# Moved norm, first-slot and band work in a two-layer decoder trunk, and two weight forms rounded in one instruction

## The reference

```
x = x + 0.5 * swiglu(rmsnorm(x, n_ffn1), w_gu, w_down)     # d_ff = 2816
x = x + mixer(rmsnorm(x, n_mix))           # layer 0: gated linear attention, layer 1: windowed means
x = x + cross_attention(rmsnorm(x, n_xattn), rmsnorm(mem, n_mem))
x = x + 0.5 * swiglu(rmsnorm(x, n_ffn2), w_gu, w_down)
```

## Time and profile before

| | |
|---|---|
| median of three runs | 1996.6 us |
| the profiled execution | 1997.72 us |
| its span, first to last instruction | 1995.6 us |
| TensorE (PE) busy | 1962.7 us, 98% |
| VectorE (DVE) busy | 1183.7 us, 59% |
| ScalarE (ACT) busy | 841.5 us, 42% |
| GpSimd (POOL) busy | 182.9 us, 9% |
| granted TensorE clock, mean | 0.995 |

### The profile page before, as it was taken

One profiled execution on the slowest core, in us unless ns is written; L12 is line 12 of the kernel. 1 busy time (PEld: TensorE's weight loads), 2 busy tenths in 40 slices (PEclk: granted clock), 3 DMA queues, 4 the chain that ended last, 5 costly groups with the idle time before them and its releaser, 6 DMA issues. The chain is left out here.

```text
span 1995.6 us, 27296 instructions
## 1 busy us (share of the span) xinstructions
PE 1962.7 (98%) x10622; PEld 1703.2 (85%) x10622; DVE 1183.7 (59%) x1595; ACT 841.5 (42%) x1249; POOL 182.9 (9%) x213
## 2 busy tenths in 40 slices
PE   9999999999999989999999899999999999999998
PEld 7888888888898878989998798899798888888887
DVE  5343343587765668947966895698487544434323
ACT  5222232265554545524544563365256443322222
POOL 2000001100112120001001100100322122200000
PEclk9999999999999999999999999999999999999999
DMA  5323352323434532333333233333353424432222
GB/s 175 105 89 100 100 143 77 102 64 106 128 126 132 164 89 80 100 100 106 105 95 106 64 105 103 98 106 100 89 185 123 106 85 127 158 105 92 97 95 74
DMA packets 250063, 214.77 MB, mean 108 GB/s; under 512 B 22802, under 2 KB 232848, under 8 KB 249984
## 3 DMA queue, kind: packets, MB, share of 16 engines
q1 hardware_dynamic: 226304, 192.95, 31.2%
q0 software_dynamic: 6432, 17.64, 3.4%
q10 hardware_dynamic: 17248, 3.16, 0.9%
HBM read 203.23 MB, written 10.49 MB: 107 GB/s over the span
## 5 line engine op out<-in xcount | busy, mean ns | idle before, releaser
L2134 DVE TENSOR_TENSOR w_lo<-raw,w_hi 128x512 fp32r<-128x512 f32 (+5 forms) x283 | 410.2, 1450 | 368.4 <-ACT w_hi L1446 368.2
L1446 ACT ACTIVATE w_hi<-raw 128x512 fp32r<-128x512 f32 (+5 forms) x283 | 344.3, 1229 | 263.9 <-PE ps L429 259.1
L427 PE MATMUL ps<-h_hi,w_hi 128*128 128x512 f32 (+1 forms) x1088 | 420.3, 386 | 0.5 <-DVE w_lo L2134 0.5
L428 PE MATMUL ps<-h_lo,w_hi 128*128 128x512 f32 (+1 forms) x1088 | 418.6, 385 | 0.0
L429 PE MATMUL ps<-h_hi,w_lo 128*128 128x512 f32 (+1 forms) x1088 | 418.1, 384 | 0.0
L427 PEld LDWEIGHTS ps<-h_hi,w_hi 128*128 128x128 f32 x1088 | 205.7, 189 | 41.1 <-DVE w_lo L2134 0.9
L429 PEld LDWEIGHTS ps<-h_hi,w_lo 128*128 128x128 f32 x1088 | 205.7, 189 | 40.7
L428 PEld LDWEIGHTS ps<-h_lo,w_hi 128*128 128x128 f32 x1088 | 205.8, 189 | 39.6
L1034 PE MATMUL ps<-s_hi,w_hi 128*128 128x256 f32 x640 | 181.5, 284 | 3.7 <-DVE ps L2235 2.0
L1035 PE MATMUL ps<-s_lo,w_hi 128*128 128x256 f32 x640 | 181.1, 283 | 0.0
L1036 PE MATMUL ps<-s_hi,w_lo 128*128 128x256 f32 x640 | 181.1, 283 | 0.0
(11 more groups left out here) (411 smaller groups left out, 3436.1 us busy)
## 6 DMA issues: line engine op xcount, KB each, us to landing
raw<-in_ffn_w_gu SPq DMA_DIRECT2D x88, 512.0 KB, 5.0
raw<-in_ffn_w_gu SPq DMA_DIRECT2D x43, 1024.0 KB, 5.1
raw<-in_ffn_w_down SPq DMA_DIRECT2D x18, 1024.0 KB, 5.1
raw<-in_x_w_kv SPq DMA_DIRECT2D x16, 1024.0 KB, 6.0
raw<-in_ffn_w_down SPq DMA_DIRECT2D x20, 768.0 KB, 4.4
raw<-in_gla_w_in SPq DMA_DIRECT2D x12, 1024.0 KB, 5.2
raw<-in_ffn_w_down SPq DMA_DIRECT2D x16, 640.0 KB, 4.2
raw<-in_x_w_q SPq DMA_DIRECT2D x8, 1024.0 KB, 5.2
```

Of the source, the lines that this page charges most:

```text
L427: nc.tensor.matmul(out_ap, left[0], right[0], start=first, stop=False)
L428: nc.tensor.matmul(out_ap, left[0], right[1], start=False, stop=False)
L1446: return nc.scalar.activation(out_ap, in_ap, ACT.Copy, **kw)
L2134: return nc.vector.tensor_tensor(out_ap, value, hi.bitcast(F32), ALU.subtract)
```

## The change

- **Norm.** In the last step of feed_last_pairs the split of the next weights and the split of the sums come first, then the sums of x.
- **First slots.** POOL's weight_sums is gone; VectorE makes these three sums (with the two plain slots in a first half, ahead of the last down pair's split for a second half). The high and low parts of the second plain slot's chunk move behind the first slot's silu. In slot 0 seed_fourth moves ahead of P1's form of the next slot.
- **Two forms in one.** w_sums is laid out anew so that P5 and P6 lie side by side; one instruction on ScalarE and one on VectorE round both (two_forms). In the other slots seed_fourth stands between sum_three and the pair. P4's form moves from place 6 to 7.
- **Ends of halves.** The first down slot is split as soon as P6 of the last slot is done (it was P2), the second after P3 (it was the last product), both earlier in the lists. The wait for low_gated moves from ahead of half_down's loop to its second block.
- **Bands.** band_split moves from ahead of the down weights to behind the second pair of them.

```diff
-    SPOT = {P1: 0, P5: 1, P6: 2, P2: 3, P7: 4, P3: 5, P4: 6}
-    SUM_OF = {P5: 0, P7: 1, P6: 2, P4: 3}
+    SPOT = {P1: 0, P5: 1, P6: 2, P2: 3, P7: 4, P3: 5, P4: 7}
+    SUM_OF = {P5: 0, P6: 1, P7: 2, P4: 3}
...
@@ gpsimd
-            weight_sums(1, 0)
-            weight_sums(1, 1)
             add_squares(4)
-            weight_sums(2, 0)
-            weight_sums(2, 1)
             bands()
@@ tensor, half_down
-                pe.wait_ge(sig.mixed_dve_step, dve_step(end - 1, C12_TAKEN))
...
+                                if (pair, g, c) == (0, 0, 1):
+                                    pe.wait_ge(sig.mixed_dve_step, dve_step(end - 1, C12_TAKEN))
@@ scalar
+            def two_forms_hi(m, done_sem, done):
+
+                w = mixed_slots[m]
+                act.wait_ge(sig.w_sum_ready, OPENED + 3 * m + SUM_STEP[P6])
+                act.wait_ge(done_sem, done)
+                hi_part(two_forms(w_hi, w), w_sums[:, 0:2]).then_inc(sig.form_hi_ready, 2)
@@ scalar, feed_last_pairs
                     feed(f, 7)
+                    split_next(split_after)
+                    sums_hi(f)
                     scale_x(f, 2)
-                    split_next(split_after)
                     x_sums_hi(f, 2)
                     scale_x(f, 3)
-                    sums_hi(f)
                     x_sums_hi(f, 3)
@@ scalar, mixed_run
                     if following:
-                        for i in (P5, P6):
-                            form_hi(m + 1, i, sig.product_done, product_count(m, i))
+                        two_forms_hi(m + 1, sig.product_done, product_count(m, P6))
...
+                    if not following:
+                        split_hi(w % 2, area[w], loaded[w], product_count(m, P6), slot_rows[w], sig.product_done)
...
+                split_hi((w + 1) % 2, area[w + 1], loaded[w + 1], product_count(m, P3), slot_rows[w + 1],
+                         sig.product_done)
                 high_silu(m, s)
-                split_hi((w + 1) % 2, area[w + 1], loaded[w + 1], OPENED + PRODUCTS * end, slot_rows[w + 1],
-                         sig.product_done)
@@ scalar and vector, mixed_ffn
-                    if (n, part) == (2, 1):
-                        band_split()
...
+                        if (n, part, pair) == (2, 1, 1):
+                            band_split()
@@ vector
+            def two_forms_lo(m):
+
+                w = mixed_slots[m]
+                dve.wait_ge(*form_hi_count(m, P6))
+                lo_part(two_forms(w_lo, w), w_sums[:, 0:2], two_forms(w_hi, w)).then_inc(sig.form_lo_ready, 2)
@@ vector, mixed_run
                         if s == 0:
+                            sum_columns(m0)
+                            sum_three(m0)
+                            sum_four(m0)
                             split_next(at["gu", n, 0].slot)
...
-                        half_mid_lo(s)
+                        if s == 0:
+                            half_mid_lo(0)
...
                     if following:
                         sum_columns(m + 1)
+                        if l == 0:
+                            seed_fourth(m, s, b)
                         form_lo(m + 1, P1)
                         sum_three(m + 1)
-                        form_lo(m + 1, P5)
-                    seed_fourth(m, s, b)
+                    if l > 0:
+                        seed_fourth(m, s, b)
                     if following:
-                        form_lo(m + 1, P6)
+                        two_forms_lo(m + 1)
...
-                    if l > 0:
-                        half_mid_lo(s - 1)
-                    high_up(m, s, b)
-                    w = mixed_slots[m] + 1
-                    if following:
+                        if l > 0 or part == 0:
+                            half_mid_lo(s - 1)
+                        high_up(m, s, b)
                         form_lo(m + 1, P7)
                     else:
                         split_lo(w % 2, area[w], w + 1, slot_rows[w])
+                        high_up(m, s, b)
+                        half_mid_lo(s - 1)
@@ vector, mixed_ffn
+                        if (part, pair) == (0, 3):
+                            sum_columns(mixed_first[n, 1])
+                            sum_three(mixed_first[n, 1])
+                            sum_four(mixed_first[n, 1])
```

More of the change, by code:

```diff
@@ L443, in form, with two_forms @@
             return flat.rearrange("p (k n) -> p k n", n=P)
+        def two_forms(parts, w):
+            spot = SPOT[P5] + 4 * area[w]
+            flat = parts[:].rearrange("p s k n -> p (s k n)")[:, spot * KH * P:(spot + 2) * KH * P]
+            return flat.rearrange("p (f k n) -> p f k n", f=2, n=P)
         def dve_step(m, step):
@@ L720, in turn_x @@
                 pool.dma_start(final_gain[:], io.n_final.unsqueeze(0).broadcast_to([P, D])).then_inc(sig.gain_loaded, 16)
[L722 to L737, removed]
             def store_o(h):
@@ L1086, in last_block @@
                 banks, _ = mixed_banks(n, part)
-                pe.wait_ge(sig.form_lo_ready, OPENED + 6 * end)
+                pe.wait_ge(sig.form_lo_ready, form_count(end, P4))
                 pe.wait_ge(sig.mixed_dve_step, dve_step(end - 1, C22_READY))
@@ L1457, in split_next @@
                     if w + 2 in mixed_slots:
-                        for i in LEADING:
-                            form_hi(mixed_slots.index(w + 2), i, sig.part_done, slot_end[w])
+                        first = mixed_slots.index(w + 2)
+                        form_hi(first, P1, sig.part_done, slot_end[w])
+                        two_forms_hi(first, sig.part_done, slot_end[w])
+                        form_hi(first, P2, sig.part_done, slot_end[w])
                         return
@@ L1521, in half_mid_hi, with plain_mid_hi @@
                     hi_part(half_hi[:, s % HALF, :], t[:, s % 2, :]).then_inc(sig.mid_hi_ready, 1)
+                def plain_mid_hi(s):
+                    act.wait_ge(sig.evacuated, at["gu", n, s].out + 2)
+                    hi_part(half_hi[:, s, :], t[:, s, :]).then_inc(sig.mid_hi_ready, 1)
                 if part == 0:
@@ L1530, in mixed_run @@
                         else:
-                            act.wait_ge(sig.w_sum_ready, OPENED + 3 * m0 + SUM_STEP[P4])
                             for i in (P7, P3):
                                 form_hi(m0, i, sig.part_done, before_run)
-                        act.wait_ge(sig.evacuated, o_gate + 2)
-                        hi_part(half_hi[:, s, :], t[:, s, :]).then_inc(sig.mid_hi_ready, 1)
+                        if s == 0:
+                            plain_mid_hi(0)
                 else:
-                    act.wait_ge(sig.w_sum_ready, OPENED + 3 * m0 + SUM_STEP[P4])
                     for i in (P7, P3):
@@ L1541, in mixed_run @@
                     m, s = m0 + l, l + (PLAIN_FIRST, HALF)[part]
-                    following = m + 1 < end
+                    following, w = m + 1 < end, mixed_slots[m] + 1
                     act.wait_ge(sig.product_done, product_count(m, P1))
@@ L1571, in mixed_run @@
                         half_mid_hi(m - 1, s - 1)
+                    elif part == 0:
+                        plain_mid_hi(1)
                     if following:
                         form_hi(m + 1, P7, sig.product_done, product_count(m, P7))
-                    else:
-                        split_hi(w % 2, area[w], loaded[w], product_count(m, P2), slot_rows[w], sig.product_done)
+                split_hi((w + 1) % 2, area[w + 1], loaded[w + 1], product_count(m, P3), slot_rows[w + 1],
+                         sig.product_done)
                 high_silu(m, s)
-                split_hi((w + 1) % 2, area[w + 1], loaded[w + 1], OPENED + PRODUCTS * end, slot_rows[w + 1],
-                         sig.product_done)
                 half_mid_hi(m, s)
@@ L2147, in split_next @@
                     if w + 2 in mixed_slots:
-                        for i in LEADING:
-                            form_lo(mixed_slots.index(w + 2), i)
+                        first = mixed_slots.index(w + 2)
+                        form_lo(first, P1)
+                        two_forms_lo(first)
+                        form_lo(first, P2)
                         return
@@ L2163, in sum_columns @@
                 dve.wait_ge(raw_loaded[w % 2], loaded[w])
-                dve.wait_ge(*form_lo_count(m - 1, P7))
-                nc.vector.tensor_tensor(w_sums[:, 0:2], *outer_columns(w), ALU.subtract).then_inc(sig.w_sum_ready, 1)
+                if m > 0:
+                    dve.wait_ge(*form_lo_count(m - 1, P7))
+                nc.vector.tensor_tensor(w_sums[:, 0:3:2], *outer_columns(w), ALU.subtract).then_inc(sig.w_sum_ready, 1)
             def sum_three(m):
                 dve.wait_ge(sig.w_sum_ready, OPENED + 3 * m + 1)
-                nc.vector.tensor_tensor(w_sums[:, 2], quarter(mixed_slots[m], 1, 1), w_sums[:, 0], ALU.subtract)\
+                nc.vector.tensor_tensor(w_sums[:, 1], quarter(mixed_slots[m], 1, 1), w_sums[:, 0], ALU.subtract)\
```

(12 more changed lines are left out.)

2 lines of the change are left out of this document (removed).

## The result

The changed kernel takes **2004.95 us** (median of five runs, 2004.38 to 2005.96) against 1996.6: ratio 1.0043 [1.0029, 1.0057], slower by 8.6 us [5.8, 11.4] (1996.6 times what the ratio is above one). Forecast were 1998.9. Its profiled execution has a span of 2003.4 us, 7.8 more than before, at a mean granted clock of 0.996.

What follows compares the result with a forecast made beforehand. TensorE, busy 98%, bounds the kernel, with VectorE close behind and becoming the slots' bound. Runs +9.8, ends of halves -3.6 and bands -3.9 sum to +2.3 us on 1996.6: 1998.9, range 1995 to 2003.

Steps and rivals of the forecast that it cites:

- The slot: In each slot, the pair's wait makes VectorE's round 10.46 us against TensorE's 10.08, a cost of 0.38 us each.
- Norms and first slots: Norm waits go, new waits replace most; P1 of slot 1 comes 2.2 us earlier in the first run, 1.8 in the second.
- the wait for P1's form: In the first slots behind the norms, TensorE now stands idle 4.4 us for this form.
- The wait for ScalarE's copy: Ahead of P6 in the first slots, TensorE stands idle 3.2 us for ScalarE's copy of bank 6.
- rival 3: In two first slots, low clock lasts through P6, delaying product and seed 0.8 to 1.2 us: 2001; chance 0.05.
- Ends and bands: Earlier splits gain 0.9 us at each of four half ends, 3.6 in all; moving the bands' split gains 3.9.
- Rival 1: In the slots, the pair's wait is hidden and TensorE stays the bound: 1985.1 us; chance 0.20.
- Rival 2: In the slots, TensorE resumes 0.4 us slower, keeping a 0.2 us wait before P3 in 32 rounds: 2005.3; chance 0.20.

## Why the prediction was wrong

**The slot.** Right in its mechanism: VectorE is the bound of the slots, through the wait of the pair. Wrong in the size of one step, "Now: sum_three 0.68 us, 0.04, the high part of 128x1024 in 1.06 us, 0.04, and only then the pair's low part: 1.82 us". The two hand-overs of 0.04 us were read from instructions that raise their counter by one. The diff has `then_inc(..., 2)` on both of the new ones, and it costs 0.05 and 0.07: 1.93 us and a round of 10.57 in place of 10.46. Over 32 rounds that is 32 x 0.11 = 3.5 us, where the range had allowed 0.05 us a round, and the kernel with the count mended is 3.9 us faster by its median. The prediction had read the diff for operations and waits, and not for what an instruction does to its counter.

**What is left.** With the count mended the sum is +2.5 us by stages, forecast +2.3. By the medians it is +4.0 (2001.06 against 1997.05), and its ratio, [1.0013, 1.0031], lies a little above the forecast's 1.0012. The execution profiled there was the fastest of its ten (1999.51), and that of the kernel before (1997.72) was 1.1 us over its median, so these two traces differ by less than the medians do. Of the 6.1 us between 1998.9 and 2004.95 some 4 are the step above; the other 2 can't be placed in a stage, and their cause stays open.

**Norms and first slots.** First gate at 754.43 us (forecast 754.3), the wait for P1's form 4.4 us, the gain of this part 4.1 us alone (forecast 2.2 + 1.8). The wait for ScalarE's copy was 1.8 us, not 3.2, because P1 and P5 ran in part at the lower clock level (0.66 from 758.40 to 763.40) and TensorE arrived later. P1 of slot 1 came at 773.33, forecast 772.2. Of these 1.1 us, 0.1 are the pair's hand-overs and some 0.35 sum_four, which waited 0.46 us behind P4's form, in the first run alone; P6, which the seed waits for, ran in part at the lower level too (0.71 from 763.40 to 768.40), and the seed waited 0.22 us for it (rival 3, in a small measure). sum_four's wait is also in the kernel with the forms apart, and not in the one with all counts one; its cause stays open.

**Ends and bands.** No wait is left at half_down, and the last P4 waits 0.37 us, forecast 0.45; last P1 to half_down 12.18 us, forecast 12.05, so 0.77 each in place of 0.9; with the ends alone, in slots of 10.08 us, it was 0.84. Bands 4.6 us, forecast 3.9.

**Rivals.** Rival 1 (slots stay TensorE's, 1985.1) is the change without its pair: 1985.3. So the sum of all other parts was right to a fraction of a microsecond, and term by term within 0.7: ends 4 x 0.84 = 3.4 us for 3.6, bands 4.6 for 3.9, norms and first slots 4.1 for 4.0. The last is in part luck, as the 2.2 and 1.8 hold 0.93 us each for the pair in slot 0, which this kernel hasn't. Rival 2 named a time of 2005.3 that came true by another mechanism: from the third slot of a run on there was no wait left before P3's low part (786.40 to 786.73 is one step of 0.33). The Trainium skill's Perfetto Trace Analysis, section Optimizing Scalar/DVE Operations, has two rules, larger operations can help where an engine is saturated, smaller ones where it isn't and makes bubbles for others; the runs side with the second by 19.7 us.

## What to carry to other kernels

Before two operations on a chain between two engines are merged, add up the chain from the last input of the merged one, not the engine's busy time: 0.07 us saved a slot brought 0.9 us of waiting, and moving one operation ahead, or merging on one engine alone, gave nearly all of it back, but no merged form was faster than the forms apart. Look in the diff at what each waiting instruction raises, too: let a merged instruction raise its counter by one and change the counts. And time the parts of a bundle apart: without the pair the change gained 11.8 us, and the pair lost 19.7.

## What the hardware showed beside

An instruction that waits and raises its counter by two starts later behind its wait than one that raises by one: 0.05 us on ScalarE (0.77 against 0.72), 0.07 on VectorE (1.16 against 1.09, and 0.48 against 0.41 on a second instruction). The traces have the wait of such an instruction in a semaphore instruction of its own, and start it 0.045 us behind the end of that. What a raise by more would cost is not shown. And removing 13.8 us of TensorE's waits was worth 4.1: 8.4 us came back as a wait for P1's form in two first slots.
